# Order of the inner rows, the last sums, the routing tables and the attention scores in a two-layer hybrid decoder trunk

## What is computed

```python
s_s = einsum(q, k_selected) * scale ; masked_softmax ; @ v      # branch 0, 8 heads of 64 channels
s_w = einsum(q, k_window)   * scale ; masked_softmax ; @ v      # branch 1
s_f = einsum(q, k) * scale + cum_q - cum_k ; masked_softmax     # branch 2 (forgetting attention)
...
for e in range(8):                                              # experts, D_FF = 2816
    out = out + gates[:, e:e + 1] * (silu(xt @ w_gate[e]) * (xt @ w_up[e])) @ w_down[e]
```

## Time and profile before

| | us |
|---|---|
| median of 3 runs | 1267.09 (1265.88 to 1267.72) |
| profiled execution, time | 1265.7 |
| profiled execution, span from the first to the last instruction | 1263.9 |
| PE busy | 1231.3 (97%) |
| DVE busy | 983.7 (78%) |
| ACT busy | 808.8 (64%) |
| attention scores and values, all 18 units | about 105.7 to 152.7 |
| experts | about 502 to 1258 |

### The profile page before, as it was taken

The page is one execution under the profiler, slowest core; times in us unless marked ns, Lnnn a source line. Parts: engine busy times, 40 slices in busy tenths (PEclk is TensorE's granted clock), DMA queues, the critical chain, the costliest instruction groups (busy, mean ns, idle before and its releaser), DMA issues.

```text
span 1263.9 us, 16135 instructions
## 1 busy us (share of the span) xinstructions
PE 1231.3 (97%) x5999; PEld 1018.8 (81%) x5999; DVE 983.7 (78%) x937; ACT 808.8 (64%) x870; POOL 60.2 (5%) x57
## 2 busy tenths in 40 slices
PE   6989999999999999999999999999999999999996
PEld 5877888888889887788888888888888888888885
DVE  4786754555556657989889889889889989989896
ACT  5454354344456554777777777777777777777773
POOL 0130000000000011310000000000000000000300
PEclk9999999999999999999999999999999999999999
DMA  9641025554444334899999999999999999999992
GB/s 370 239 150 51 2 100 200 200 200 180 176 155 157 133 122 163 266 421 402 389 390 367 392 391 365 401 375 367 404 375 368 404 375 368 389 374 369 401 394 98
DMA packets 52041, 361.58 MB, mean 286 GB/s; under 512 B 5984, under 2 KB 6112, under 8 KB 9728
## 3 DMA queue, kind: packets, MB, share of 16 engines
q1 hardware_dynamic: 48720, 349.54, 71.6%
q0 software_dynamic: 3248, 11.03, 2.3%
HBM read 354.76 MB, written 5.78 MB: 285 GB/s over the span
## 4 chain that ended last, share of the span: by engine, by line
PE 89%; DVE 7%; issue 1%; ACT 1%; DMA 1%; POOL 1%; SPq 0%; DVEq 0%; ACTq 0%
PE bank L559 26%; PE bank L561 26%; PE bank L560 26%; DVE wlo L1977 2%; PE bank L1048 1%; PE bank L748 1%; PE bank L774 1%; DVE wlo L1432 1%; PE bank L907 1%; PE bank L756 1%; ACT whi L1130 1%; DMA raw<-in_weights 1%; PE bank L569 1%; PE bank L1013 0%; PE bank L711 0%
## 5 line engine op out<-in xcount | busy, mean ns | idle before, releaser
L1977 DVE TENSOR_TENSOR wlo<-raw,whi 128x2048 fp32r<-128x2048 f32 x261 | 597.7, 2292 | 69.5 <-ACT whi L1366 61.7
L1366 ACT CAST whi<-raw 128x2048 fp32r<-128x2048 f32 x261 | 499.1, 1912 | 114.1 <-PE bank L561 113.5
L559 PE MATMUL bank<-whi,hT_hi 128*128 128x512 f32 (+1 forms) x1104 | 431.6, 391 | 9.7 <-DVE wlo L1432 7.2
L561 PE MATMUL bank<-whi,hT_lo 128*128 128x512 f32 (+1 forms) x1104 | 429.5, 389 | 0.0
L560 PE MATMUL bank<-wlo,hT_hi 128*128 128x512 f32 (+1 forms) x1104 | 429.0, 389 | 0.0
L559 PEld LDWEIGHTS bank<-whi,hT_hi 128*128 128x128 f32 x1104 | 207.8, 188 | 53.4 <-issue 7.6
L561 PEld LDWEIGHTS bank<-whi,hT_lo 128*128 128x128 f32 x1104 | 207.8, 188 | 43.0
L560 PEld LDWEIGHTS bank<-wlo,hT_hi 128*128 128x128 f32 x1104 | 207.9, 188 | 41.9
L1432 DVE TENSOR_TENSOR wlo<-raw,whi 128x2048 fp32r<-128x2048 f32 x68 | 155.7, 2291 | 100.2 <-ACT whi L1130 99.4
L1130 ACT CAST whi<-raw 128x2048 fp32r<-128x2048 f32 x68 | 129.9, 1912 | 101.0 <-PE bank L561 99.0
L559 PE MATMUL bank<-whi,h_hi 128*128 128x512 f32 x440 | 181.3, 412 | 0.0
(11 more groups left out here) (299 smaller groups left out, 815.8 us busy)
## 6 DMA issues: line engine op xcount, KB each, us to landing
raw<-in_weights SPq DMA_DIRECT2D x329, 1024.0 KB, 5.7
sums<-ybuf POOLq DMA_DIRECT2D x7, 512.0 KB, 5.1
arena<-in_compress SPq DMA_DIRECT2D x1, 1088.0 KB, 14.0
x<-in_x SPq DMA_DIRECT2D x2, 512.0 KB, 5.9
tokens<-hng POOLq DMA_DIRECT2D x2, 512.0 KB, 3.4
out<-x SPq DMA_DIRECT2D x2, 512.0 KB, 4.1
cst<-in_constants SPq DMA_DIRECT2D x1, 603.0 KB, 11.2
picks<-in_norm_row POOLq DMA_DIRECT2D x1, 512.0 KB, 5.4
```

The costliest lines, as they stand in the source:

```text
L559: mm(out_, a_hi, b_hi, start=start, stop=False)
L561: return mm(out_, a_lo, b_hi, start=False, stop=stop)
L1366: nc.scalar.copy(whi[:, u % SPLIT, :, :], raw[:, u % RAW, :, :]).then_inc(S["w_hi"], 1)
L1977: V.tensor_tensor(wlo[:, u % SPLIT, :, :], raw[:, u % RAW, :, :], whi[:, u % SPLIT, :, :].bitcast(F32), ALU.subtract).then_inc(S["w_lo"], 1)
```

## The change

There are six edits.

1. Attention: `qT` and `keyT` get two more rows of zeros (two POOL memsets ahead of everything else it does; PE waits for them before qk(0)), branches 0 and 1 multiply over 66 rows, and the mask comes after the heads of a unit and covers only the 128 columns of each head that it changes: 512 columns for t = 0, 256 for t = 1. The mask tensor shrinks from 288 KB to 160 KB.
2. In the last chunk of every expert (c = 10), ACT's `hidden_turned(9)` and DVE's `hidden_lower(9)` stand ahead of a weight unit and not behind it.
3. The last down unit of expert 7 goes by column halves, a new semaphore `first_half` lets `final_sums` start on the first half, `scatter` and `scattered` go by halves, and x is stored in four DMAs of half the columns.
4. The first instruction of `overflow` stands ahead of a weight split; the rest of `overflow` moves to chunk 6 of expert 0.
5. `positions` moves from chunk 0 to chunk 3 of expert 0.
6. The four `combine` move from chunks 6, 7, 8, 9 of expert 7 to chunks 4, 6, 8 and behind the last `hidden_lower`.

```diff
-                mm(b[:, :], mident, msk[:, 512 * t:512 * t + 512], start=True, stop=False)
                 for j in range(n):
                     if br < 2:
-                        q, k = qT[0:HD, h, t * P:(t + 1) * P], keyT[0:HD, br * 2 + h // 4, 0:kw]
+                        q, k = qT[0:66, h, t * P:(t + 1) * P], keyT[0:66, br * 2 + h // 4, 0:kw]
-                    last = mm(b[:, j * kw:(j + 1) * kw], q, k, start=False, stop=(j == n - 1))
-                last.then_inc(S["scores"], 1)
+                    mm(b[:, j * kw:(j + 1) * kw], q, k, start=(j == 0), stop=False)
+                own_keys = b[:, :].rearrange("p (h n) -> p h n", h=n)[:, :, t * P:(t + 1) * P]
+                mm(own_keys, mident, msk[:, 0:n * P].rearrange("p (h n) -> p h n", h=n), start=False, stop=True)\
+                  .then_inc(S["scores"], 1)
...
@@ POOL
+            link(nc.gpsimd.memset(qT[HD:66, :, :], 0.0))
+            link(nc.gpsimd.memset(keyT[HD:66, :, :], 0.0))
             norm(0)
@@ PE, scatter and m_down
-                    t, half = i // 2, i % 2
-                    if i < 2:
+                    half, t = i // 2, i % 2
+                    if t == 0:
                         pe.wait_ge(S["ysb"], kth * 2 + half + 1)
...
-                    for j in range(2):
-                        for half in range(2):
+                    for a in range(2):
+                        for b in range(2):
+                            j, half = (b, a) if c == NCH - 1 else (a, b)
...
+                        if c == NCH - 1 and a == 0:
+                            last.then_inc(S["first_half"], 1)
@@ ACT (DVE likewise with hidden_lower)
+                    if c == NCH - 1:
+                        hidden_turned(c - 1)
                     split_unit(pos_g(c, 1, fresh) + SPLIT)
-                    if c or not fresh:
+                    if (c or not fresh) and c < NCH - 1:
                         hidden_turned(c - 1)
@@ DVE, expert
-                        if c == 0:
+                        if c == 3:
                             positions()
+                        if c == GATHER:
+                            overflow()
...
-                    if drain and not fresh and c in (6, 7, 8, 9):
-                        combine((c - 6) // 2, c % 2)
+                    if drain and not fresh and c in (4, 6, 8):
+                        combine((c - 4) // 4, c // 2 % 2)
...
                 if drain:
                     hidden_lower(NCH - 1)
+                    if not second:
+                        combine(1, 1)
                     sums_lower(e - NE + 1)
@@ DVE, ahead of expert 0
+            dve.wait_ge(S["count"], 1)
+            link(V.tensor_scalar(over[:, 0, :], bank[2][:, 0:8], float(CAP), None, ALU.is_gt))
             split(U_MOE + 2)
-            overflow()
@@ SP
-            for t in range(NT):
+            for i, (half, t) in enumerate(product(range(2), range(NT))):
+                c = slice(half * BLK, (half + 1) * BLK)
-                sp.wait_ge(S["x_ready"], n_over * 4 + (X_MOE + 8 - 2 * (NT - 1 - t)))
-                sp.dma_start(out_d[t * P:(t + 1) * P, :], x[:, t, :]).then_inc(S["out"], 16)
+                sp.wait_ge(S["x_ready"], n_over * 4 + (X_MOE + 5 + i))
+                sp.dma_start(out_d[t * P:(t + 1) * P, c], x[:, t, c]).then_inc(S["out"], 16)
```

More of the change, by code:

```diff
@@ L22 @@
 from contextlib import ExitStack
+from itertools import product
 import concourse.bass as bass
@@ L146, in masks @@
     i = np.arange(P)
-    m = np.zeros((P, 1024 + P), np.float32)
+    m = np.zeros((P, 512 + P), np.float32)
     late = np.where(i[:, None] >= i[None, :], 0.0, NEG)
@@ L150, in masks @@
         m[:, h * P:(h + 1) * P] = late
-    m[:, 512 + 128:512 + 256] = late
-    m[:, 512 + 384:512 + 512] = late
-    m[:, 1024:1024 + P] = np.eye(P)
+    m[:, 512:512 + P] = np.eye(P)
     return (m.view(np.uint32) >> 16).astype(np.uint16)
@@ L174, in trunk @@
         cst = sb("cst", [P, C_END])
-        msk_bits = sb("msk_bits", [P, 1024 + P], mybir.dt.uint16)
+        msk_bits = sb("msk_bits", [P, 512 + P], mybir.dt.uint16)
         msk = msk_bits[:, :].bitcast(BF16)
@@ L208, in trunk @@
         iota = cst[:, C_IOTA:C_IOTA + P]
-        mident = msk[:, 1024:1024 + P]
+        mident = msk[:, 512:512 + P]
         bank = [ctx.enter_context(nc.psum_tensor(f"bank{i}", [P, 512], F32)) for i in range(8)]
@@ L353, in trunk @@
             combT_psum combT xg_psum xg cur m_silu m_hact m_h2T_psum m_h2T ysb scat out
-            norm_row zeroed tables_zero hng tokens_out table_at table_out slot_token rows_even rows_odd y_out y_stored sums_at picks_in""".split()
+            norm_row zeroed tables_zero hng tokens_out table_at table_out slot_token rows_even rows_odd y_out y_stored sums_at picks_in first_half""".split()
         S = {n: sem(n) for n in NAMES}
@@ L466, in _ @@
                                      .rearrange("a p (b n) -> p (a b) n", b=UB)).then_inc(s_loaded[sl], 16)
-            for t in range(NT):
-                sp.wait_ge(S["x_ready"], n_over * 4 + (X_MOE + 8 - 2 * (NT - 1 - t)))
-                sp.dma_start(out_d[t * P:(t + 1) * P, :], x[:, t, :]).then_inc(S["out"], 16)
-            sp.wait_ge(S["out"], NT * 16)
+            for i, (half, t) in enumerate(product(range(2), range(NT))):
+                c = slice(half * BLK, (half + 1) * BLK)
+                sp.wait_ge(S["x_ready"], n_over * 4 + (X_MOE + 5 + i))
+                sp.dma_start(out_d[t * P:(t + 1) * P, c], x[:, t, c]).then_inc(S["out"], 16)
+            sp.wait_ge(S["out"], 2 * NT * 16)
         @block.gpsimd
@@ L778, in _ @@
             pe.wait_ge(S["foxT"], 8)
+            pe.wait_ge(S["pool_chain"], 3)
             qk(0)
@@ L1349, in store_sums, with final_sums @@
                     nc.scalar.copy(ybuf[:, half * BLK:(half + 1) * BLK], bank[4 + half][:, :]).then_inc(S["y_out"], 1)
-            def final_sums(e, used):
-                act.wait_ge(S["units_used"], used)
+            def final_sums(kth, used):
                 for half in range(2):
+                    if half == 0:
+                        act.wait_ge(S["first_half"], kth + 1)
+                    else:
+                        act.wait_ge(S["units_used"], used)
                     A(y_hi[:, half * BLK:(half + 1) * BLK], bank[4 + half][:, :], ACT.Copy, scale=gslot[:, 0:1])\
@@ L1397, in expert @@
                     hidden_turned(NCH - 1)
-                    final_sums(e, (e + 1) * EXP_UNITS + U_MOE)
+                    final_sums(e - NE + 1, (e + 1) * EXP_UNITS + U_MOE)
             for half in range(2):
@@ L1893, in overflow @@
                 R = OVER_ROUNDS
-                dve.wait_ge(S["count"], 1)
-                link(V.tensor_scalar(over[:, 0, :], bank[2][:, 0:8], float(CAP), None, ALU.is_gt))
                 link(V.tensor_tensor_scan(over[:, 1, :], ones[:, 0:8], over[:, 0, :], 0.0, ALU.mult, ALU.add))
@@ L1995, in expert @@
                                     bank[(par + c) % 2][:, CH:2 * CH], ALU.mult).then_inc(S["m_hact"], 1)
+                    if c == NCH - 1:
+                        hidden_lower(c - 1)
                     split_unit(pos_g(c, 1, fresh) + SPLIT)
-                    if c or not fresh:
+                    if (c or not fresh) and c < NCH - 1:
                         hidden_lower(c - 1)
                     if fresh and not drain:
-                        if c == 0:
+                        if c == 3:
                             positions()
+                        if c == GATHER:
+                            overflow()
                         if c == TURN + 1:
```

## The result

| | median, us | lowest to highest | executions |
|---|---|---|---|
| before | 1267.86 | 1265.88 to 1269.80 | 12 |
| after | 1271.55 | 1269.05 to 1275.88 | 12 |

A forecast was written before the change was run, and what follows sets the result against it. The prediction took PE, busy 97% of the span, as the bound. Attention -4.2, expert 0 +5.2, expert 7's combine +3.5 and the end -3.8 sum to +0.7 us: 1267.8 us for the median, range 1262.0 to 1271.0.

The forecast's parts named there:

- the rows' wait: Expert 0: with `positions` in chunk 3, PE waits for the gathered rows of expert 1 and starts `turn_rows` 5.2 us later.
- the gather's 9.1 us: Expert 0: the gather of expert 1's rows takes 9.1 us to land, as before; up to 14.6 us as bound.
- rival on that chain: Expert 0's table DMAs: either 5 us shorter, so expert 0 costs nothing (chance 0.20), or longer (chance 0.17).
- the rival of the longer chain: Expert 0: the gather takes up to 14.6 us in place of 9.1, sum up to +6.2 us; chance 0.17.
- The picks' wait: Expert 7, chunk 4: DVE's `combine` waits for the last gather of picks; PE gets `wlo` 3.5 us late.
- The bound of 5 us: Expert 7: upper bound on the cost of the moved `combine`, taken as +3.5 us with bounds +1.5 and +5.
- The gains: The two terms that save time: attention 4.2 us and the end of expert 7 3.8 us.
- attention: 66 rows and narrower masks save 5.4 us, less 0.9 at the start and 0.3 at the end: 4.2 us.
- the last turn: End of expert 7: PE's 2.2 us wait for `hidden_lower` ahead of it goes; with its restart -2.3 us.
- the column halves: End of expert 7: from last matmul to last add 4.0 us in place of 4.9, so -0.9 us.
- The store: End of expert 7: half the bytes behind the last add save 0.6 us, bounds 0 and 1.3.
- The carry to the median: The sum against the profiled execution (1265.7 us) is carried to the median, 1267.1 us, 1.4 us above it.

The follow-up runs named there:

- x16: The change as it is, run again beside x14 on the same chip: 1271.25 us.
- x2b: The same kernel as x2, run again beside one whose rows' wait is filled: 1265.96 us.
- x2: The change with the first three `combine` in chunks 6, 7 and 8 of expert 7, the fourth still behind the last `hidden_lower`: 1265.10 us.
- x1: The change with `positions` back in chunk 0 of expert 0: 1265.39 us.
- x13: The change with `positions` in chunk 2 in place of 3, `combine` staying in chunk 4: 1263.56 us.
- x14: The change with useless mask matmuls in both waits, 20 ahead of the rows' turn in expert 0 and 16 ahead of the waiting down units in expert 7: 1268.46 us.
- x7: The kernel before with only the scores of branches 0 and 1 over 66 rows, mask still first and 512 columns wide: 1264.62 us.
- x3: The change with `positions` back in chunk 0 and the first three `combine` in chunks 6, 7 and 8: 1259.94 us.
- x8: The kernel before with only the mask last and over the own keys' columns, scores still over 64 rows: 1264.93 us.
- x4: The kernel before with the whole attention edit alone, 66 rows and the smaller mask last: 1263.12 us.

## Why the prediction was wrong

- **Waits were priced at their length.** This is the step that failed: "PE ... starts `turn_rows` at 568.5 and not at 563.3: 5.2 us" and "gets it 3.5 us late ... nothing more is lost". Behind either wait PE runs at 1.2 GHz for a while. By the yardstick this was 1.6 us (after), 2.3 (x16), 2.5 (x2b) and 2.9 (x2) behind the rows' wait, and 1.8 (x16, x1), 1.9 (x13) and 2.6 (after) behind the picks'. The filled waits show it as a cause, with 1.65 us for the one and 2.8 for both.
- **The rows' wait itself** came as worked out. The chain from `positions` to the landing took 35.8 us in before (513.06 to 548.9) and 35.5 us in after (529.53 to 564.98), so taking the gather's 9.1 us was right (8.86 here), and no rival on that chain came in. There is some luck in it: in x14, with `positions` at the same place, the landing was 2 us later, which is the rival of the longer chain, and with `positions` in chunk 0 the chain takes 38.5 us in x7. PE started `turn_rows` 4.2 us later than before, counted from the dispatch (565.0 - 495.9 = 69.1 against 563.3 - 498.4 = 64.9), where 5.2 were forecast. Medians: 6.2 us for 5.2, of which some 2 are the clock's; so the wait itself came out about 1 us shorter than forecast, and the clock more than made up for it.
- **The picks' wait** was 2.9 us on PE in x16 and 7.35 in the profiled execution of after, for 3.5 forecast. The prediction took POOL's first gather to start as in before. It hangs on the landing of the store of `sums`, which POOL waited 5.0 us for in before and x16, and 9.8 us in after; over the 17 traces of this study that wait is 4.8 to 6.0 us in eleven, 7.0 in one and 8.7 to 9.8 in five, whatever the kernel. This may also widen the spread of the times, which is not shown: x13, which waits for the picks, spreads over 2.6 us, and x2, which doesn't, over 6.3. The bound of 5 us was too near. Medians: 6.4 us (5.5 against x3, 4.6 in x13) for 3.5.
- **The gains** came as summed: 8.0 for 8.0 (x3). In parts: attention 3.9 by trace for 4.2 (152.56 - 107.42 against 154.70 - 105.70 from the first score unit to the first output matmul), with a wait of 0.44 us at turn(0) for 0.7; the last turn 2.4 us for 2.3, and the column halves 1.0 for 0.9. The store gave 0 for 0.6; and 1.6 us that the prediction had not, the slow matmuls behind the last turn, go with the 2.2 us wait in most executions. So the agreement is luck in part: the parts add to 3.9 + 2.4 + 1.0 + 1.6 = 8.9 us, and the 0.9 us to the medians' 8.0 is not explained.
- **The carry to the median** was wrong for the same reason. The 1.4 us by which the median lies above the profiled execution were taken as a constant. The cost of the clock behind the last turn, which the profiled execution of before did not pay (1.00 there) and which the change removes, is enough for all of it: with that wait filled the median is 1265.67 us. But the profiled execution of before was also the earliest of the 17 at the start of attention (last section), so the split is not shown.

The sum: 2.9 us too little for the two waits, and the median of before, 1267.86 over 12 executions and not 1267.09 over 3, makes 0.8. Together 3.7 us, which is the miss (1271.55 - 1267.8). What can't be told from these runs is why the store of `sums` lands in about 5 or about 9 us; a kernel in which only its place among the weight loads changes was not tried.

## What to carry to other kernels

Price a wait of PE, when PE is the busiest engine, at its length plus what the clock takes behind it, here 1.6 to 2.9 us behind waits of 2.2 to 7.4 us (and nothing behind the 2.2 us wait in two traces of four); a wait of 2 us can nearly double. Work that only has to meet a deadline is free to move up to it, but the slack must be counted in the slowest landing seen, not in the one of the profiled execution: `positions` one chunk earlier and `combine` two chunks later turn this change from 3.7 us slower to 8.7 us faster, with 0.7 us in hand in the tighter of two traces. Where a wait can't be removed, useless matmuls in it bring back the clock's part (1.8 us in the kernel before), as long as they fill it.

## What was not expected of the hardware

- The granted clock falls behind short waits in some executions and not in others: behind the 2.2 us wait it was 1.00 in before and x8 and went down to 0.68 and 0.52 in x7 and x4.
- The stretch ahead of attention varies too, and no run tells why. The clock is 0.50 to 0.52 from 95 to 100 us in every trace, but from 100 to 105 us it is 0.91 in before, 0.58 in after, and 0.71 and 0.88 in two executions of one and the same kernel (x2 and x2b). The first score unit starts at 105.70 us in before, at 106.01 and 107.42 in two executions of the change (x16 and after). x2, then x2b:

```profile
100.00:105.00 5.00, 4.48 (x27) 3.81 (x26) 1.49 (x5) 4.10 (x8) 0.00 (x0) 0.71 0.07 30
```

```profile
100.00:105.00 5.00, 4.48 (x29) 3.56 (x28) 1.45 (x5) 3.88 (x8) 0.00 (x0) 0.88 0.23 95
```

- A store of 512 KB from POOL's queue, among weight loads at a DMA share of 0.95 to 1.00, lets POOL go on after 4.8 to 6.0 us or after 8.7 to 9.8 us, with one of the 17 between (7.0).
